# A transformer block in one kernel: the scan's running sum as a bias of ScalarE, and a mixer's first chunks token by token

## The reference, cut to what matters

```python
def odd_mixer(h, ...):
    proj = h @ w_in                       # 1024 -> 4128 columns
    g = glu_a * jax.nn.sigmoid(glu_b)     # 512 channels
    g = depthwise_conv(g, dw_w, dw_b, ...)        # 31 taps
    g = jax.nn.silu(layer_norm(g, ln_g, ln_b))
    xbc = jax.nn.silu(depthwise_conv(xbc, conv_w, conv_b, ...))   # 4 taps, 2048 channels
    dt = jax.nn.softplus(dt_raw + dt_bias)
    A = -jnp.exp(A_log)
    y_f = ssd_scan(xs, dt[:, :, 0], A[0], Bm, Cm)
    y_b = flip(ssd_scan(flip(xs), flip(dt[:, :, 1]), A[1], flip(Bm), flip(Cm)))
    y = y_f + y_b + xs * D_skip
    y = rms_norm(y * jax.nn.silu(z), norm_w)
    return jnp.concatenate([g, y], axis=-1) @ w_out
```

## Time and profile before

| | us |
|---|---|
| median of 3 executions | 2992.65 |
| profiled execution | 2992.17 |
| its span | 2990.3 |
| TensorE busy | 2826.2 (95%) |
| VectorE busy | 1941.1 (65%) |
| ScalarE busy | 1468.2 (49%) |
| GpSimd busy | 119.4 (4%) |
| sublayer 10 in the trace | 2563 to 2794 |

### The profile page before, as it was taken

One profiled execution on the slowest core, in us unless ns is written; L12 is line 12 of the kernel. 1 busy time (PEld: TensorE's weight loads), 2 busy tenths in 40 slices (PEclk: granted clock), 3 DMA queues, 4 the chain that ended last, 5 costly groups with the idle time before them and its releaser, 6 DMA issues.

```text
span 2990.3 us, 36273 instructions
## 1 busy us (share of the span) xinstructions
PE 2826.2 (95%) x14172; PEld 2343.6 (78%) x14172; DVE 1941.1 (65%) x2519; ACT 1468.2 (49%) x2172; POOL 119.4 (4%) x121
## 2 busy tenths in 40 slices
PE   5999989979999999999998899999999999899999
PEld 4887878757888888878786688787778788787787
DVE  7788786676778797775535554655665554586654
ACT  4454453476454454544545644544554444474543
POOL 0000000000000000000040000000000000172000
PEclk9999999999999999999999999999999999899999
DMA  8567674205677677975642255554355465440553
GB/s 322 205 229 274 228 244 142 105 1 209 241 243 264 213 274 266 298 236 185 225 148 71 90 207 189 191 183 155 124 196 183 169 211 184 153 153 18 188 185 127
DMA packets 100553, 562.75 MB, mean 188 GB/s; under 512 B 20256, under 2 KB 20768, under 8 KB 43936
## 3 DMA queue, kind: packets, MB, share of 16 engines
q1 hardware_dynamic: 100384, 560.43, 53.5%
HBM read 559.30 MB, written 1.09 MB: 187 GB/s over the span
## 4 chain that ended last, share of the span: by engine, by line
PE 79%; DVE 8%; ACT 6%; DMA 3%; issue 3%; SPq 0%; DVEq 0%; ACTq 0%
PE banks L359 24%; PE banks L361 24%; PE banks L360 24%; PE banks L835 2%; DVE w_rest L346 1%; ACT w_high L336 1%; DVE ada_terms L432 1%; DMA post_mod<-post_scale 1%; PE banks L658 1%; ACT normed L677 1%; DMA ada_tiles<-in_w_ada 1%; DVE post_term L539 1%; PE banks L1256 1%; DVE ada_terms L390 1%; PE banks L1521 1%
## 5 line engine op out<-in xcount | busy, mean ns | idle before, releaser
L346 DVE TENSOR_TENSOR w_rest<-w_raw,w_high 128x2048 fp32r<-128x2048 f32 x426 | 976.1, 2293 | 551.1 <-ACT w_high L336 550.6
L336 ACT ACTIVATE w_high<-w_raw 128x2048 fp32r<-128x2048 f32 x426 | 810.7, 1907 | 240.9 <-PE banks L361 198.5
L359 PE MATMUL banks<-w_high,u_parts 128*128 128x512 f32 (+1 forms) x2160 | 829.8, 384 | 35.3 <-DVE post_term L539 16.4
L361 PE MATMUL banks<-w_high,u_parts 128*128 128x512 f32 (+1 forms) x2160 | 817.7, 379 | 0.0
L360 PE MATMUL banks<-w_rest,u_parts 128*128 128x512 f32 (+1 forms) x2160 | 816.7, 378 | 0.0
L359 PEld LDWEIGHTS banks<-w_high,u_parts 128*128 128x128 f32 x2160 | 411.3, 190 | 109.8 <-issue 23.8
L361 PEld LDWEIGHTS banks<-w_high,u_parts 128*128 128x128 f32 x2160 | 411.0, 190 | 76.4
L360 PEld LDWEIGHTS banks<-w_rest,u_parts 128*128 128x128 f32 x2160 | 411.6, 191 | 70.9
L359 PE MATMUL banks<-w_high,gated_high 128*128 128x512 f32 x968 | 379.3, 392 | 4.8 <-DVE w_rest L346 4.1
L361 PE MATMUL banks<-w_high,gated_rest 128*128 128x512 f32 x968 | 376.9, 389 | 0.0
L360 PE MATMUL banks<-w_rest,gated_high 128*128 128x512 f32 x968 | 376.7, 389 | 0.0
(11 more groups left out here) (288 smaller groups left out, 2740.0 us busy)
## 6 DMA issues: line engine op xcount, KB each, us to landing
w_raw<-in_w_ffn_in SPq DMA_DIRECT2D x242, 1024.0 KB, 4.9
w_raw<-in_w_ffn_out SPq DMA_DIRECT2D x121, 1024.0 KB, 5.0
ada_tiles<-in_w_ada SPq DMA_DIRECT2D x128, 512.0 KB, 5.0
w_raw<-in_w_mix SPq DMA_DIRECT2D x54, 1024.0 KB, 5.0
w_raw<-in_w_mix_out SPq DMA_DIRECT2D x22, 1024.0 KB, 5.0
ada_first<-in_w_ada SPq DMA_DIRECT2D x7, 1024.0 KB, 16.6
post_gain_row<-post_mod SPq DMA_DIRECT2D x10, 512.0 KB, 6.6
na_bias<-in_na_bias SPq DMA_DIRECT2D x1, 4096.0 KB, 14.1
```

The source lines that it names most:

```text
L336: act.activation(w_high(g)[:, 0:n], raw[:, g % RING, 0:n], ACT.Copy).then_inc(w_hi_ready, 1)
L346: nc.vector.tensor_tensor(w_rest(g)[:, 0:n], raw[:, g % RING, 0:n], w_high(g)[:, 0:n].bitcast(F32), ALU.subtract).then_inc(w_lo_ready, 1)
L359: nc.tensor.matmul(ps, hi_a, hi_b, start=first_, stop=False)
L361: return nc.tensor.matmul(ps, lo_a, hi_b, start=False, stop=last_)
```

## The change

1. `hand_over_pe` turns only the first token tile in sublayer 10. Chunks 0 and 1 have tokens as rows: `first_pe` computes chunk 0 and five of eight parts of chunk 1 for the first token tile, then the second tile is turned, then the rest follows. The GLU of these chunks is formed token by token (sigmoid and product in halves of 128 x 128), turned by TensorE (`turn_glu`, two transposes a chunk) and copied by VectorE.
2. `cumulate` stands behind chunk 14 and waits for seven pairs of the short convolution. It also forms the sums with tokens as rows (eight products of 16 columns), which VectorE negates into `cols`. The sums for `exponent` are kept in two parts, with one instruction each on ScalarE and VectorE.
3. `exponent` leaves out the six products for -a[s]; ScalarE adds it as the bias of exp, one column of `cols` for each of four PARTS, so a head has four exps in place of one. VectorE's maps are one instruction of 512 columns and two of 128. y takes four products.
4. PRODUCTS has 31 entries in place of 42, so GpSimd multiplies 29 of its 60 later steps itself, in place of 18.

The core of the diff:

```diff
         def hand_over_pe(s):
 turn_pe(s, 0, 0)
-if s == 10:
-    turn_pe(s, 0, 1)
         def hand_over_act(s):
 TAPS_BESIDE = [0, 0, 6, 8, 10, 6, 5, 2, 2, 2, 2, 2, 2, 2, 2, 6, 5]
 FIRST_PAIR = 7
+PRODUCTS_BESIDE = [0, 0, 0, 5, 6, 6, 1, 1, 1, 1, 1, 1, 1, 1, 2, 2, 2]
...
+    if e < 4:
+        return self.sem["glu_tokens"], e + 1
     return (self.sem["glu"], e // 2 + 1) if e < 8 else (proj_taken, self.base + e - 8 + 1)
+def first_pe(self, pe, c, tt, kts):
+    g = self.proj.g0 + c
+    tok = slice(tt * P, (tt + 1) * P)
+    await_rest(pe, g)
+    await_u(pe, 10, 0, tt)
+    if c == 1 and tt == 0:
+        pe.wait_ge(y_taken, 4 * PASSES.index((9, 0)) + 4)
+    for k in kts:
+        cols = slice(k * CHUNK, (k + 1) * CHUNK)
+        ins = three(bank[2 * c + tt][:, 0:CHUNK], u[:, 0, 0, k, tok], w_high(g)[:, cols], u[:, 0, 1, k, tok],
+                    w_rest(g)[:, cols], k == 0, k == KT - 1)
+    if kts[-1] == KT - 1:
+        ins.then_inc(w_used if tt else self.sem["half_chunk"], 1)
+def turn_glu(self, pe, c):
+    S = self.sem
+    pe.wait_ge(S["glu_tokens"], 2 * c + 2)
+    for tt in range(2):
+        ins = pe.transpose(bank[7 - c][:, tt * P:(tt + 1) * P], self.x[:, c, tt * P:(tt + 1) * P], ident[:])
+    ins.then_inc(S["glu_turned"], 1)
...
     for c in range(17):
         highs(g0 + c + LEAD)
-        if c == 13:
+        if c == 15:
             act.wait_ge(S["cum_ready"], 1)
             act.activation(self.cum[:], bank[7][:], ACT.Copy).then_inc(S["cum_high"], 1)
...
+        if c < 2:
+            for tt in range(2):
+                if tt:
+                    act.wait_ge(w_used, g0 + c + 1)
+                else:
+                    act.wait_ge(S["half_chunk"], c + 1)
+                act.activation(ta[:, c, tt * P:(tt + 1) * P], bank[2 * c + tt][:, P:CHUNK], ACT.Sigmoid)\
+                    .then_inc(S["sigmoid"], 1)
+            continue
         act.wait_ge(w_used, g0 + c + 1)
...
-        if c == 14:
-            act.wait_ge(S["cum_left"], 1)
-            act.activation(self.mid[64:96], self.left[64:96], ACT.Copy).then_inc(S["cum_mid"], 1)
-            act.activation(self.cum[32:64], self.left[32:64], ACT.Copy).then_inc(S["cum_mid"], 1)
...
         act.wait_ge(S["exponent"], hh + 1)
         if hh >= 2:
             act.wait_ge(S["maps"], hh - 1)
-        act.activation(self.seg[:, hh % 2], self.exponents(hh)[:, 0:6 * P], ACT.Exp).then_inc(S["decay"], 1)
+        act.wait_ge(S["cum_columns"], 1)
+        for way, st, (a, b), _ in self.PARTS:
+            ins = act.activation(self.seg[:, hh % 2, a:b], self.exponents(hh)[:, a:b], ACT.Exp,
+                                 bias=self.cols[:, way, st, hh:hh + 1])
+        ins.then_inc(S["decay"], 1)
...
-        if c < 4:
+        if c < 2:
+            for tt in range(2):
+                dve.wait_ge(S["sigmoid"], 2 * c + tt + 1)
+                dve.tensor_tensor(self.x[:, c, tt * P:(tt + 1) * P], bank[2 * c + tt][:, 0:P],
+                                  ta[:, c, tt * P:(tt + 1) * P], ALU.mult).then_inc(S["glu_tokens"], 1)
+        if 1 <= c < 3:
             dve.wait_ge(S["pads"], 4)
-            dve.wait_ge(S["sigmoid"], c + 1)
+            dve.wait_ge(S["glu_turned"], c)
+            dve.tensor_copy(self.gp[:, c - 1, CONV_K // 2:CONV_K // 2 + SEQ], bank[8 - c][:, 0:SEQ])\
+                .then_inc(S["glu"], 1)
+        if 2 <= c < 4:
+            dve.wait_ge(S["sigmoid"], c + 3)
             dve.tensor_tensor(self.gp[:, c, CONV_K // 2:CONV_K // 2 + SEQ], bank[2 * c % 4][:, 0:SEQ],
                               ta[:, c % 2, 0:SEQ], ALU.mult).then_inc(S["glu"], 1)
...
+                for n in range(2):
                     dve.scalar_tensor_tensor(self.a3[:, m, :, 32 * n:32 * n + SSM_H],
...
-        if c == 13:
+        if c == 15:
+            dve.wait_ge(S["cum_ready"], 1)
+            dve.tensor_scalar(self.cols[:].rearrange("p a b c -> p (a b c)"), bank[5][:, 0:4 * SSM_H], -1.0,
+                              None, ALU.mult).then_inc(S["cum_columns"], 1)
             dve.wait_ge(S["cum_high"], 1)
-            dve.tensor_tensor(self.left[:], bank[7][:], self.cum[:].bitcast(F32), ALU.subtract)\
-                .then_inc(S["cum_left"], 1)
-        if c == 15:
-            dve.wait_ge(S["cum_mid"], 2)
-            dve.tensor_tensor(self.cum[64:96], self.left[64:96], self.mid[64:96].bitcast(F32), ALU.subtract)\
+            dve.tensor_tensor(self.cum[32:64], bank[7][32:64], self.cum[32:64].bitcast(F32), ALU.subtract)\
                 .then_inc(S["cum_split"], 1)
...
-        dve.tensor_tensor(blocks(m[:, of]), blocks(seg[:, of]), blocks(cb)[:, 0:4:3], ALU.mult)\
-    dve.tensor_tensor(m[:, 4 * P:], seg[:, 4 * P:], cb[:, P:3 * P], ALU.mult).then_inc(S["maps"], 1)
+    dve.tensor_tensor(wide(m)[:, 0:3:2], wide(seg)[:, 0:3:2], wide(cb), ALU.mult).then_inc(S["maps_cut"], 1)
+    dve.tensor_tensor(m[:, SEQ:SEQ + P], seg[:, SEQ:SEQ + P], cb[:, SEQ + P:], ALU.mult)\
+        .then_inc(S["maps_cut"], 1)
+    dve.tensor_tensor(m[:, SEQ + P:BOTH], seg[:, SEQ + P:BOTH], cb[:, 0:P], ALU.mult).then_inc(S["maps"], 1)
...
-    for c in range(17):
+    self.first_pe(pe, 0, 0, range(KT))
+    self.first_pe(pe, 1, 0, range(5))
+    turn_pe(10, 0, 1)
+    self.first_pe(pe, 1, 0, range(5, KT))
+    self.first_pe(pe, 0, 1, range(KT))
+    self.first_pe(pe, 1, 1, range(KT))
+    self.turn_glu(pe, 0)
+    for c in range(2, 17):
         self.proj.pe_chunk(c)
-        if c == 12:
+        if c == 2:
+            self.turn_glu(pe, 1)
+        if c == 14:
             self.cumulate(pe)
...
             pe.wait_ge(S["y_taken"], kt - 1)
-        m = self.m[:, hh % 2].rearrange("p (b n) -> p b n", n=P)
-        pe.matmul(bank[kt % 2][r, 0:SEQ].rearrange("p (b n) -> p b n", n=P),
-                  self.xdt[0][:, 0, hh * HD:(hh + 1) * HD], m[:, 0:5:4], start=True, stop=False)
-        for n in (1, 2, 3, 5):
-            way, st, lt = self.BLOCKS[n]
-            ins = pe.matmul(bank[kt % 2][r, lt * P:(lt + 1) * P],
-                            self.xdt[way][:, st, hh * HD:(hh + 1) * HD], m[:, n], start=False, stop=n == 5)
+        for n, (way, st, (a, b), (l0, l1)) in enumerate(self.PARTS):
...
     pe.wait_ge(const_landed, 16 * self.const)
-    pe.wait_ge(S["a_ready"], 6)
-    pe.wait_ge(S["conv"], 6 * 6)
+    pe.wait_ge(S["a_ready"], 4)
+    pe.wait_ge(S["conv"], 6 * 7)
     for way in range(2):
         for kt in range(2):
             ins = pe.matmul(bank[7][:, way * SEQ:(way + 1) * SEQ], self.a3[:, kt, way], self.sums[:, way, kt],
                             start=kt == 0, stop=kt == 1)
+    for way in range(2):
+        for st in range(2):
+            o = (2 * way + st) * SSM_H
+            for kt in range(2):
+                ins = pe.matmul(bank[5][:, o:o + SSM_H], self.sums[:, way, kt, st * P:(st + 1) * P],
+                                self.a3[:, kt, way, 0:SSM_H], start=kt == 0, stop=kt == 1)
     ins.then_inc(S["cum_ready"], 1)
...
-    pe.matmul(to[:, 0:4 * P], this.to_broadcast([P, P]), self.cum[:], start=False, stop=False)
-    pe.matmul(to[:, 4 * P:6 * P], this.to_broadcast([P, P]), self.cum[:, P:3 * P], start=True, stop=False)
-    for n, (way, st, lt) in enumerate(self.BLOCKS):
-        ins = pe.matmul(to[:, n * P:(n + 1) * P], self.cum[:, way * SEQ + st * P:way * SEQ + (st + 1) * P],
-                        less.to_broadcast([P, P]), start=False, stop=n in (3, 5))
-    ins.then_inc(S["exponent"], 1)
+    this = self.pick[:, hh:hh + 1].to_broadcast([P, P])
+    pe.matmul(to[:, 0:BOTH], self.eye[:], self.cut[:].rearrange("p b n -> p (b n)"), start=True, stop=False)
+    pe.matmul(to[:, 0:SEQ], this, self.cum[:, 0:SEQ], start=False, stop=False)
+    pe.matmul(to[:, SEQ:BOTH], this, self.cum[:, P:3 * P], start=False, stop=True)
+    pe.matmul(to[:, BOTH:3 * SEQ], this, self.cum[:, SEQ:BOTH], start=True, stop=False)
+    pe.matmul(to[:, 3 * SEQ - P:3 * SEQ], self.eye[:], self.cut[:, 3], start=False, stop=True)\
+        .then_inc(S["exponent"], 1)
 def out(self, pe):
```

50 lines of the change are left out of this document (22 added, 28 removed).

## The result

| | before | after |
|---|---|---|
| median of 5 executions, us | 2991.37 (2985.50 to 2992.88) | 2974.89 (2972.76 to 2975.16) |
| ratio, with its 95% interval | 1 | 0.9948 (0.9937 to 0.9960) |
| profiled execution: time, span | 2992.17, 2990.3 | 2975.16, 2973.3 |
| sublayer 10, from its first transposes to those of sublayer 11 | 230.46 | 213.04 |

The change makes the kernel faster: by 16.5 us between the medians, by 17.0 between the profiled executions, by 17.4 inside sublayer 10. Forecast were 18.2 us and 2974.0.

A forecast was written before the change was run, and what follows sets the result against it. TensorE, busy 95% of the span, was taken to bound the kernel. The terms -5.5 - 6.4 - 3.6 - 5.8 + 1.6 + 1.5 = -18.2 us gave 2974.0 us, range 2966 to 2984.

The forecast's parts named there:

- Hand-over, -5.5: Start of sublayer 10: first transposes to chunk 1's sigmoid get 5.5 us shorter, taking the form of sublayer 7.
- The bound of -8: Lower limit of the hand-over estimate at the start of sublayer 10: 8 us saved if there is no half clock.
- cumulate, -6.4: Moving cumulate behind chunk 14: TensorE's 7.00 us wait for VectorE's short convolution goes, 6.4 us saved.
- Start of the scan, -3.6: First heads: VectorE's last taps end earlier and the clock doesn't fall, 3.6 us more saved.
- Exponents, -5.8: Scan heads: an exponent takes 0.82 us in place of 1.40; ten on the path save 5.8 us.
- Four exps, +1.6: End of the scan: four exps a head in place of one cost ScalarE 1.6 us over heads 13 to 15.
- GpSimd, +1.5: Head 6: TensorE waits for GpSimd, which has 13 steps of its own in place of eight; 1.5 us lost.
- Both clocks: Forecast times at head 6, hand-over left out: GpSimd's 13 steps end at 2712.9, TensorE wants them at 2711.1.
- The rival, that maps block GpSimd fully: Scan: GpSimd steps cost near 2.5 us beside VectorE's maps, TensorE waits 10 us at head 6, total 2982; chance 0.15.
- The clock in the scan: Rival for the scan: short exponent products bring TensorE to half clock, 36 us over 16 heads, total 3010; chance 0.04.

The follow-up runs named there:

- changed again: The changed kernel run once more as it is, for a second trace; ratio to before 0.9943, sublayer 10 takes 210.35 us.
- cum12: Changed kernel with the sums of cumulate behind chunk 12 again, waiting for six convolution pairs; bias-column products stay behind chunk 14; ratio to before 0.9957.
- one_exp: Changed kernel with one exp of 768 columns and no bias in place of four, subtraction of a[s] left out; ratio to before 0.9938.
- bias_undone: Changed kernel with six products subtracting a[s] again, one exp, maps and y by blocks, no bias columns; ratio to before 0.9936.
- products42: Changed kernel with the 42 products by ScalarE of before; ratio to before 0.9926.
- ln_late: Changed kernel with layer norm's silu and copies behind head 15's exps, scaling behind head 14's maps, rest parts behind head 15's maps; ratio to before 0.9923.
- reorder: Changed kernel with C . B of the first two groups ahead of the exponent of head 1; ratio to before 0.9943.
- best: Changed kernel with 42 ScalarE products, C . B ahead of head 1's exponent, layer norm's silu behind head 15's exps, scaling behind its maps; 0.9917 of before, 2962.46 us.
- best2: Kernel of best with the last square of y between the layer norm's second and third silu, ahead of the root's table load; ratio to before 0.9930.
- best8: Kernel of best with all eight parts of chunk 1 for the first token tile ahead of the second tile's transposes, not five; ratio to before 0.9921.

## Why the prediction was right, and where it was off

The time came out 0.9 us beside the forecast, and the mechanisms are those named; that the sum fits so closely is luck, since larger misses of its terms cancel. It also rests on the falls of the clock in the first trace: in "changed again" sublayer 10 is 20.1 us shorter than before, not 17.4. The steps:

- **Hand-over, -5.5: direction right, too small by 2.1.** I took the form of sublayer 7 as it stood, with 6.6 us near half clock, and added 0.4 for `turn_glu`. Here the half clock lasted 3.6 us in the first trace, and eight of twelve traces have none. Where the clock stays up, the sigmoid comes 8.5 us earlier than before. The bound of -8 was nearer.
- **cumulate, -6.4: right.** B measured -6.6, with the 0.3 of `turn_glu` in it, and cum12 6.4. The 3.42 us of `cumulate` were forecast as 3.7. TensorE never waited for w_rest in chunks 13 to 16.
- **Start of the scan, -3.6: too large by 1.0 us, with the first two y by 1.7.** From the exponent of head 0 to that of head 2 it is 11.22 before and 8.61 after, -2.6. The exponent of head 1 came 0.9 us nearer to that of head 0 (3.51, now 2.57), not 1.5. The wait ahead of head 1 (1.78, forecast 1.5) and the clock came as forecast. What I had missed is the wait at the exponent of head 2, which grew from 0.96 to 1.51 us, since it waits for the exps of head 0; and the first two y wait 1.11 us for maps in place of 0.36.
- **Exponents, -5.8: the size right (0.57 us each), the count not.** Seven exponents, of heads 2 to 8, stand between the start of the scan and head 6, not five; behind head 6 five more stand ahead of the root, as forecast. The two more are worth 1.1 us and cover a part of what the start of the scan lacks. TensorE came to head 6 at 26.9 us behind the exponent of head 0, where the forecast comes to 26.0 (2711.1 less 2685.1), and still came ahead of GpSimd.
- **Four exps, +1.6: mis-sized, measured +2.4.** The exps themselves were 0.54 us longer, as forecast (1.35 us; the forecast took 1.4). From the figures of the Trainium skill (ScalarE: Activation LUTs, What ACT_TABLE_LOAD costs) the estimate for the four is 1.48; the trace is 0.13 below. Of the 2.4 us, 1.2 are longer waits (forecast 1.6), and 1.2 are the clock, which fell behind a wait of 3.04 us and which one_exp and bias_undone don't show behind 1.88 us.
- **GpSimd, +1.5: measured +2.75, and 2.56 by products42.** Both clocks ran late. Behind the exponent of head 0 GpSimd was to end at 27.8 us (2712.9 less 2685.1) and ended at 29.5: its 13 steps began at 3.6 in place of 3.0, and took 1.99 us each in place of 1.91. TensorE was 0.9 us late too, or the wait would have been longer. The rival, that maps block GpSimd fully, falls: a multiplication beside maps takes 1.48 or 1.61 us in place of 0.93, beside a rest part 2.96 or more before and after. The Trainium skill (GPSIMD Engine Reference, Key points) names contention with VectorE instructions with two SBUF inputs. The trace agrees, and shows that short VectorE instructions cost a multiplication of GpSimd up to 0.7 us; many beside maps took 0.92 to 1.08.
- **The clock in the scan: right.** It stayed at 1.00 in the heads; short products as such did not bring it down. Where it fell, in this and in the other traces, TensorE was waiting or had waited just before.

A trap was that the sum was right while its parts moved against each other: the hand-over 2.1 better, the scan 3.1 worse. And a statement on the whole change hides that two of its four points earned nothing as put together: the bias cost 0.2 us, fewer products by ScalarE 2.6.

## What to carry to other kernels

Time saved on the bounding engine counts only up to its next wait for another engine, and a longer wait there can cost more than it was, since the clock may fall behind it: list the places where it meets another engine, and count each saving up to the nearest of them. When several edits each show no gain alone, look whether they meet the same wait before they are dropped: three of them gave 5.2 us together (with the scaling of the layer norm one place further back) where alone one gave 2.6 and the others cost 0.6 and 2.8. With repeated executions this uneven, distances between two events inside the changed stage tell 0.2 us where times of the whole tell 5, as long as the clock fell at the same places in both traces; a fall that only one of them has shifted the distance by 0.8 to 3.2 us.

## What the runs showed of the hardware

- The same instructions, with the same waits ahead of them, ran at full or at half clock from one execution to the next: the sigmoid behind chunk 1 at 20.27 or 21.11 us, the dt chunk 5.43 or 6.27 to 7.84 us, head 6's products 1.97 or 3.75 us behind a wait of 2.75 us each time. Of TensorE's waits behind the start of the scan, all eleven of 3.03 to 4.30 us had a fall of the clock within them or right behind, and so had one of four of 2.75 us. Of shorter ones some were and some weren't: at the last y the clock stayed up behind 1.88 us (before, one_exp, bias_undone) and fell behind 2.13 (ln_late) and 1.77 us (cum12); behind 1.92 us at the last but one it fell in cum12 and stayed up in six other traces; at the first heads it fell behind two of 0.95 and 1.02 to 1.04 us (reorder, best, best2, best8), and stayed up behind two of 0.96 and 1.12 us (one_exp). So the length of the last wait alone does not decide.
- Without any wait of TensorE the clock fell in all fourteen traces in or right behind the dt chunk, whose 48 matmuls have 32 columns: from 2.7 us behind its first product (best2) to 0.4 us behind its end (seven traces fell only behind it), and stayed down for 3.4 to 10.2 us.
- At full clock the eight products in full precision of 16 columns took 0.21 us each (1.70 us in all, from 2664.50), half of one of 256 columns (0.43). In the dt chunk a matmul of 32 columns took 0.11 us, in the other chunks one of 256 took 0.12: an eighth of the columns saved a twelfth of the time.
